# An S5, attention and convolution backbone step: S products in row halves with q slabs between, K and Y in column halves, the adaLN gate by DMA

## The reference, cut to what matters

```python
shift, scale, gate = split(silu(cond) @ w_ada + b_ada)
h = rmsnorm(x) * (1 + scale) + shift
z = h @ w_in                     # conv, ssm, q, k, v, gates, merge
br_a = (conv_module(z) * silu(conv_gate)) @ w_conv_out     # depthwise conv, width 31
# S5: 32 groups of 16 channels, 64 complex states, two directions
hs = scan(lam_bar, b_bar @ u);  y = d * u + real(c @ hs)
br_b = (glu(gelu(y)) * silu(ssm_gate)) @ w_ssm_out
br_c = (attention(qnorm(q), knorm(k), v) * silu(attn_gate)) @ w_attn_out
x = x + gate * ((g_a*br_a + g_b*br_b + g_c*br_c) @ w_out)
```

## Time and profile before

| what | value |
| --- | --- |
| median of 3 runs | 691.57 us (690.62 to 692.12) |
| profiled execution | 691.89 us, span 690.1 us |
| TensorE busy | 643.8 us, 93% |
| VectorE busy | 535.7 us, 78% |
| ScalarE busy | 309.6 us, 45% |
| GpSimd busy | 80.4 us, 12% |
| mean granted clock of TensorE | 0.989 |

### The profile page before, as it was taken

How to read it: one execution, slowest core, us unless ns; L and a number is a source line. 1 busy time by engine, 2 the same in 40 slices (tenths; PEclk the granted TensorE clock), 3 DMA queues, 4 the chain that set the end, 5 groups by cost and what they waited for, 6 DMA issues and landing times.

```text
span 690.1 us, 9683 instructions
## 1 busy us (share of the span) xinstructions
PE 643.8 (93%) x3573; PEld 460.7 (67%) x3573; DVE 535.7 (78%) x996; ACT 309.6 (45%) x534; POOL 80.4 (12%) x81
## 2 busy tenths in 40 slices
PE   3699799998999999999999899999999999989997
PEld 1377674554745688877887587465565578878885
DVE  2669889996676967789966837999767799987663
ACT  2665350540545354444546636044256544445441
POOL 2100220147000000010001710012700000010000
PEclk9999999999999999999999999999999999999999
DMA  7991817654583655655443337570443345655531
GB/s 263 373 315 58 264 60 230 238 186 119 174 284 120 180 160 173 183 162 153 162 149 113 116 137 267 179 258 29 151 151 106 106 127 184 199 163 181 184 102 61
DMA packets 67307, 117.66 MB, mean 171 GB/s; under 512 B 11052, under 2 KB 15484, under 8 KB 67260
## 3 DMA queue, kind: packets, MB, share of 16 engines
q1 hardware_dynamic: 66980, 116.94, 52.9%
q10 hardware_dynamic: 280, 0.11, 0.1%
HBM read 112.51 MB, written 1.38 MB: 165 GB/s over the span
## 4 chain that ended last, share of the span: by engine, by line
PE 72%; DVE 12%; SPq 6%; ACT 3%; issue 3%; DMA 2%; POOL 1%; ACTq 0%; POOLq 0%; DVEq 0%
PE proj L816 19%; PE proj L844 11%; PE proj L846 11%; PE proj L845 11%; PE side L831 4%; PE side L987 3%; PE side L974 2%; PE side L1068 2%; DVE raw_split L1506 2%; PE long L786 2%; PE side L1016 2%; SPq L629 1%; PE proj L786 1%; PE side L1066 1%; DMA raw<-in_w_in 1%
## 5 line engine op out<-in xcount | busy, mean ns | idle before, releaser
L816 PE MATMUL proj<-raw,hT 128*128 128x512 f32 (+1 forms) x320 | 132.0, 558 | 0.0
L1609 DVE SCALAR_TENSOR_TENSOR cvacc<-cvpad,taps,cvacc 128x256 f32<-128x256 f32 x240 | 99.0, 478 | 0.2
L816 PEld LDWEIGHTS proj<-raw,hT 128*128 128x128 f32 x320 | 58.2, 190 | 58.8 <-issue 57.0
L1212 ACT ACTIVATE wide_split<-raw 128x1024 fp32r<-128x1024 f32 x56 | 58.7, 1060 | 56.2 <-PE proj L846 56.2
L1506 DVE TENSOR_TENSOR raw_split<-raw,wide_split 128x1024 fp32r<-128x1024 f32 x56 | 67.8, 1221 | 17.2 <-ACT wide_split L1212 16.5
L845 PE MATMUL proj<-raw_split,H_split 128*128 128x512 f32 x192 | 75.5, 393 | 0.0
L844 PE MATMUL proj<-wide_split,H_split 128*128 128x512 f32 x144 | 57.9, 402 | 4.2 <-DVE raw_split L1506 4.2
L846 PE MATMUL proj<-wide_split,H_split 128*128 128x512 f32 x144 | 56.9, 395 | 0.0
L1212 ACT ACTIVATE utok_split<-raw 128x1024 fp32r<-128x1024 f32 x28 | 29.6, 1058 | 34.5 <-PE proj L846 34.5
L1506 DVE TENSOR_TENSOR raw_split<-raw,utok_split 128x1024 fp32r<-128x1024 f32 x28 | 34.2, 1221 | 12.3 <-ACT utok_split L1212 12.3
L2010 POOL TENSOR_SCALAR st<-st 128x1 f32<-128x1 f32 x8 | 4.6, 571 | 332.5 <-DVE st L1924 251.8
(11 more groups left out here) (255 smaller groups left out, 1377.6 us busy)
## 6 DMA issues: line engine op xcount, KB each, us to landing
raw<-in_w_in SPq DMA_DIRECT2D x104, 512.0 KB, 4.5
raw<-in_w_ada SPq DMA_DIRECT2D x48, 512.0 KB, 5.4
raw<-in_w_out SPq DMA_DIRECT2D x16, 512.0 KB, 3.8
raw<-in_w_ssm_glu SPq DMA_DIRECT2D x8, 512.0 KB, 7.1
raw<-in_w_ssm_out SPq DMA_DIRECT2D x8, 512.0 KB, 3.8
raw<-in_w_attn_out SPq DMA_DIRECT2D x8, 512.0 KB, 4.2
raw<-in_w_conv_out SPq DMA_DIRECT2D x8, 512.0 KB, 3.7
raw<-in_w_in SPq DMA_DIRECT2D x8, 256.0 KB, 3.6
```

The lines of the kernel that those rows point to most:

```text
L816: m = T.matmul(proj.bank((l, u, s))[:, 0:n], lhs[:, s, kt, :], w[:, i, :], start=(kt == 0), stop=last)
L1212: S.activation(piece_room[m], piece_raw(m), ACT.Copy).then_inc(piece_hi, 1)
L1609: m = V.scalar_tensor_tensor(acc, src, taps[:, t, j:j + 1], acc, ALU.mult, ALU.add)
```

## The change

S becomes one product per group: 64 rows of `E` against the 64 columns of its own group, the even group in the upper half of the rows and the odd one in the lower, into two banks at a time. Behind each of the first three pairs of banks TensorE works one slab of q and its ada slab; the q stage keeps the last. K and Y put groups in the two halves of the output partitions, K in four banks instead of eight. HY makes all four quarters before Y, the last two in `tA` and `tB`. The counts of taps per place change. The gate third of the adaLN output is no longer transposed: GpSimd adds the bias in row form (`gaterow`), and SP spreads the rows over 128 partitions by DMA into `th`; the bias comes by two DMAs into `taprow`, ahead of the q slabs in SP's queue. The waits that go with these places change too: b_loads wait for Y, `adaE` waits for `gaterow`, `bbar` for the last gate load, and GpSimd clears `taprow` at the start.

```diff
@@ -48,11 +48,11 @@
 EARLY = ("cg", "ssm", "ca")
 LATE_ROOMS = 3
 
-TAPS_IN_ZONE = (26, 14)
-TAPS_IN_Y = (8, 5, 6)
+TAPS_IN_ZONE = (22, 12)
+TAPS_IN_Y = 12
 TAPS_IN_ATT = (((8, 8, 4, 4, 2), (4, 4, 4, 4, 0)), ((6, 6, 3, 3, 2), (4, 4, 4, 4, 0)))
 
-CONV_B = (12, 18)
+CONV_B = (14, 20)
 
 LAST_COMB = ("comb", BRANCHES[-1], 1)
 
@@ -75,9 +75,9 @@
                  ("bbar", l), ("unit", "ca"), ("pack",)]
     return (begin
             + [("UT",), ("S",), ("cp",), ("bz", 0), ("convT", 0), ("convT", 1), ("unit", "q"), ("unit", "kv"), ("adaE", l, 2),
-               ("K", 0), ("sumsq", 0), ("sumsq", 1), ("unit", "sg"), ("bz", 1), ("K", 1), ("scan", 0, NCHUNK), ("HY",),
-               ("unit", "ag")] + nxt("adaE", n, 0)
-            + [("qkn",), ("conv", TAPS_IN_ZONE[l], None), ("Y",), ("adaT", l, 2)] + nxt("adaT", n, 0)
+               ("K", 0), ("sumsq", 0), ("sumsq", 1), ("bz", 1), ("unit", "sg"), ("K", 1), ("gaterow",), ("scan", 0, NCHUNK),
+               ("HY",), ("unit", "ag")] + nxt("adaE", n, 0)
+            + [("qkn",), ("conv", TAPS_IN_ZONE[l], None), ("Y",)] + nxt("adaT", n, 0)
             + [("qkT", 0), ("qkT", 1), ("att", 0)] + nxt("adaE", n, 1)
             + [("geT",), ("att", 1), ("unit", "glub"), ("unit", "glua"), ("split", 0), ("split", 1)]
...
@@ -319,12 +318,15 @@
         HY, HYs = shared("HY", [P, 2, 8, 2, NS, NCHUNK])
         HYf = HY[:, :, :, :, :, :].rearrange("p a g r s k -> p a (g r s k)")
         Ug = HY[0:NS * NCHUNK].rearrange("p a g r s k -> p (a g r s k)")
+        states = [HY[:, 0], HY[:, 1]] + [t[:, :].rearrange("p (g r s k) -> p g r s k", g=8, r=2, s=NS) for t in (tA, tB)]
         geT = HYf[:, 0, :].rearrange("p (s t q) -> p s t q", s=NS, t=WT)
         utok, utoks = shared("utok", [P, NS, W])
         cvpad = sb("cvpad", [P, WT, NS, P + 2 * PAD])
         cvacc, cvaccs = shared("cvacc", [P, WT, NS, P])
         taps = sb("taps", [P, WT, TAPS + 1])
         taprow = sb("taprow", [P, W])
+        biasrow = taprow[:, 0:ADA_W]
+        gaterow = bzf[:, 0:ADA_W]
         rows = sb("rows", [P, 3, W])
         modrow = rows[:, 0, 0:P]
...
@@ -647,9 +655,27 @@
 
             def tap_loads(l):
                 if l:
-                    side.filled(sp, ("taps", l - 1))
+                    sp.wait_ge(gaterow_done, l)
                 sp.dma_start(taprow[0:TAPS, :], A["conv_dw_w"][l]).then_inc(taps_in, 16)
                 sp.dma_start(taprow[TAPS:TAPS + 1, :], A["conv_dw_b"][l:l + 1, :]).then_inc(taps_in, 16)
+
+            def bias_loads(l):
+
+                side.filled(sp, ("taps", l))
+                for s in range(NS):
+                    sp.dma_start(biasrow[s::P // ADA_TILES, :],
+                                 A["b_ada"][l, 2 * D:3 * D].rearrange("(j x) -> j x", x=ADA_W)).then_inc(bias_in, 16)
+
+            def gate_rows(l, h):
+
+                sp.wait_ge(gaterow_done, l + 1)
+                for s in range(NS):
+                    key = (l, "gate" + str(h), s)
+                    th_claim(sp, key)
+                    for i in range(2):
+                        row = P // ADA_TILES * (2 * h + i) + s
+                        sp.dma_start(th_view(key)[:, ADA_W * i:ADA_W * i + ADA_W],
+                                     gaterow[row:row + 1, :].unsqueeze(1).to_broadcast([1, P, ADA_W])).then_inc(gate_in, 16)
 
             def c_loads(l):
...
@@ -745,6 +772,8 @@
                         b_loads(l + 1)
                         c_loads(l + 1)
                         tap_loads(l + 1)
+                    if stg[0] == "wout" and i == 3:
+                        gate_rows(l, stg[1])
                     if n >= first:
                         slab(n)
...
@@ -964,28 +993,34 @@
                     side.drained(pe, ("E", l, 5))
                     side.drained(pe, ("E", l, 6))
                     side.drained(pe, ("E", l, 7))
-                    for i in range(8):
-                        key = ("S", l, i)
-                        side.claim(pe, key)
-                        out = side.bank(key)[:, :].rearrange("p (g a r q) -> p g r a q", g=2, a=2, r=2)
-                        for gg in range(2):
-                            gp = 2 * i + gg
+                    for i in range(4):
+                        keys = [("S", l, 2 * i + a) for a in range(2)]
+                        for key in keys:
+                            side.claim(pe, key)
+                        for gp in range(4 * i, 4 * i + 4):
                             for r in range(2):
-                                m = T.matmul(out[:, gg, r, :, :], E[:, r, gp, :], Uz[:, 2 * gp:2 * gp + 2, :],
-                                             start=True, stop=True)
-                        m.then_inc(side.full, 1)
+                                for a in range(2):
+                                    at = 64 * (2 * (gp % 4) + r)
+                                    m = T.matmul(side.bank(keys[a])[:, at:at + 64], E[64 * a:64 * a + 64, r, gp, :],
+                                                 Uz[64 * a:64 * a + 64, 2 * gp + a, :], start=True, stop=True)
+                                    if gp == 4 * i + 3 and r == 1:
+                                        m.then_inc(side.full, 1)
+                        if i < 3:
+                            for key in [(l, "q", i)] + riders(l, "q", i):
+                                slab_work(key)
                 elif k == "K":
                     half = stg[1]
                     pe.wait_ge(cp_done, 2 * (l + 1))
                     pe.wait_ge(bz_done, 2 * l + half + 1)
-                    for i in range(4 * half, 4 * half + 4):
+                    for i in range(2 * half, 2 * half + 2):
                         key = ("K", l, i)
                         side.claim(pe, key)
                         for b in range(4):
-                            g = 4 * i + b
                             for r in range(2):
-                                m = T.matmul(side.bank(key)[0:48, 80 * b:80 * b + 80], bz[:, r, g % 16, :],
-                                             CP[:, r, :, g, :], start=(r == 0), stop=(r == 1))
+                                for a in range(2):
+                                    g = 8 * i + 4 * a + b
+                                    m = T.matmul(side.bank(key)[64 * a:64 * a + 48, 80 * b:80 * b + 80], bz[:, r, g % 16, :],
+                                                 CP[:, r, :, g, :], start=(r == 0), stop=(r == 1))
                         m.then_inc(side.full, 1)
                 elif k == "qkT":
                     s = stg[1]
@@ -1060,13 +1095,15 @@
                         side.claim(pe, key)
                         pe.wait_ge(hy_fwd, 4 * l + q + 1)
                         pe.wait_ge(hy_bwd, 4 * l + q + 1)
-                        for gi in range(8):
-                            g = 8 * q + gi
-                            o = side.bank(key)[0:64, 64 * gi:64 * gi + 64]
-                            T.matmul(o, Uz[:, g, :], M[:, :, g // 2, :], start=True, stop=False)
+                        for i in range(4):
+                            gs = [4 * q + i, G // 2 + 4 * q + i]
+                            out = [side.bank(key)[64 * a:64 * a + 64, 64 * i:64 * i + 64] for a in range(2)]
+                            for a in range(2):
+                                T.matmul(out[a], Uz[:, gs[a], :], M[:, :, gs[a] // 2, :], start=True, stop=False)
                             for r in range(2):
-                                m = T.matmul(o, HY[:, q % 2, gi, r, :, :].rearrange("p s k -> p (s k)"),
-                                             CP[:, r, 1:L + 1, g, :], start=False, stop=(r == 1))
+                                for a in range(2):
+                                    m = T.matmul(out[a], states[q][:, 4 * a + i, r, :, :].rearrange("p s k -> p (s k)"),
+                                                 CP[:, r, 1:L + 1, gs[a], :], start=False, stop=(r == 1))
                         m.then_inc(side.full, 1)
                     key = ("fin", l)
...
@@ -1092,17 +1129,6 @@
                     for t in range(WT):
                         m = transpose(side.bank(key)[:, P * t:P * t + P], src[:, P * t:P * t + P])
                     m.then_inc(side.full, 1)
-                if k == "wout":
-                    h = stg[1]
-                    side.drained(pe, ("adaT", l, 2))
-                    for s in range(NS):
-                        key = ("gate", l, h, s)
-                        side.claim(pe, key)
-                        for i in range(4):
-                            col = ada[:, l, 2 * DT + 4 * h + i, s:s + 1]
-                            m = T.matmul(side.bank(key)[:, P * i:P * i + P], col.to_broadcast([P, P]), ident[:, :],
-                                         start=True, stop=True)
-                        m.then_inc(side.full, 1)
                 if k == "pass":
                     u, s, h = stg[1:]
...
@@ -1187,8 +1213,8 @@
 
             def states_fwd(q):
 
```

(73 more changed lines are left out.)

51 lines of the change are left out of this document (27 added, 24 removed).

## The result

The changed kernel takes 739.05 us (737.15 to 739.5, 4 executions) against 691.85 for the kernel before in the same measurement: ratio 1.068, 95% interval [1.065, 1.070]. Forecast were 698.3 us and a range of 690.8 to 712.6. The sign was right; the size was off by 41 us, and nearly all of that is one term, the gates by DMA.

What follows compares the result with a forecast made beforehand. The prediction took TensorE (72% of the chain) as the bound, with VectorE taking over between S and attention. Terms 0.8 + 0.4 + 5.0 + 3.2 + 2.8 - 5.5 = +6.7 us gave a 698.3 us median, range 690.8 to 712.6.

Steps and rivals of the forecast that it cites:

- Gates by DMA: In both `wout` stages, TensorE's gate products and ScalarE's copies vanish: -5.5 us, bounds 2.9 to 7.2.
- S itself: S in row halves: 64 pairs at 112 ns, 7.2 us, unchanged, if row halves overlap as column tiles do.
- (a): Rival on S: half-row loads follow one another, S takes 14.3 us, +14.2, so 712.5 us; chance 0.16.
- (b): Rival on S: half-row products with their loads cost half, S 3.6 us, -7.2, so 691.1 us; chance 0.10.
- The 0.4 us for the bias loads: Layer 0: bias loads ahead in SP's queue make the first q slab late: +0.4 us, bounds 0 and 1.
- `cp` 13.5 us later behind S's start: Slabs inside S (12.6 us) and one more drain (0.9 us) delay VectorE's `cp` products in each layer.
- VectorE's taps set the first scores: Taps run unbroken to 182 and 510, TensorE idling 8 us or more; first scores +0.8 and +5.0 us.
- GpSimd caught by the taps: GpSimd's k norm product of stream 1 ends only with VectorE's taps; the norm's rest then takes 2.1 us.
- K and Y count nothing: Column halves of K and Y are covered by VectorE's chain: 0 us; without cover up to 10 a layer.
- The clock: TensorE's idle before stream 1's transposes brings one clock dip in each attention: +3.2 us, bounds 0 and 6.8.
- rival (c): The waits are there, but the clock holds and the rooms absorb the taps: 692.3 us; chance 0.14.
- Taps in the branches: Layer 1's branches take more taps, 3.6 us less VectorE's idle: +2.8 us, bounds 0 and 3.6.

Runs made afterwards that it cites:

- ky_halves_dram: The kernel before with K and Y in column halves and the gates by DMA from rows written to DRAM first: 674.53 us (0.976).
- ky_halves_only: The kernel before with K and Y in column halves, with the four state copies in a row this needs, and nothing else: 679.51 us (0.983).
- via_dram: The changed kernel with the gate rows first written to DRAM and spread over 128 partitions from there: 703.74 us (1.017).
- pe_gate: The changed kernel with the gates made by TensorE and copied by ScalarE as before, all other edits kept: 704.64 us (1.018).
- own_row: The changed kernel with each gate load reading source row p for target row p, not one row for all 128: 703.26 us (1.015).
- s_whole_between: The changed kernel with gates by TensorE and S at full height, q slabs still between its pairs of banks: 699.14 us (1.011).
- s_first: The changed kernel with gates by TensorE and the three q slabs behind S instead of between its pairs: 696.88 us (1.008).
- before_dma_gate: The kernel before with the gates by DMA alone, nothing else changed: 721.65 us (1.044).
- s_between_only: The kernel before with S in row halves, q slabs between its pairs and the changed tap numbers; K and Y full width, gates by TensorE: 709.94 us (1.025).
- s_halves_only: The kernel before with S in row halves alone, its pairs one behind the other: 714.2 us (1.033).
- taps_back: The changed kernel with gates by TensorE and the kernel before's numbers of taps, q slabs still inside S: 713.81 us (1.032).
- s_first_taps: The changed kernel with gates by TensorE, q slabs behind S and the kernel before's numbers of taps: 698.41 us (1.009).

## Why the prediction was wrong

**The step that failed** is in "Gates by DMA": SyncE "issues four loads, some 0.6 us each, ahead of one w_out slab, which still lands before ScalarE asks for it". The median issue was 0.60 us, but landing took 7.2 to 21.4 us, and the slab came 11.4 us after ScalarE asked. The term was -5.5; in the changed kernel it is +34.4 (739.05 - 704.64). I had priced the loads by their issue and never asked how long they hold the DMA engines. The trace of before had no load with a single source partition in SBUF; that made it a cost to bound from both sides, and I bounded only the gain, 2.9 to 7.2. Its own `rows<-in_ssm_d` spreads a DRAM row over 128 partitions, 256 KB landing in 3.2 us, and was no row for this one.

**The gain of 5.5 itself** was too large by a little, as far as the runs tell. Where the source is not the fault, ky_halves_dram against ky_halves_only has 5.0 us, with intervals that overlap; via_dram against pe_gate has 0.9, own_row 1.4, though in both S of layer 1 ran under a dip of 6.8 us that pe_gate's did not. The two stretches that hold a `wout` are, added up, 4.6 us shorter in via_dram's profile than in pe_gate's, and 4.5 shorter in ky_halves_dram's than in ky_halves_only's.

**S itself: right.** 16 pairs take 2.00 us at full clock, 125 ns a pair against 112 (before, 115 an instruction):

```profile
97.84 2.00 PE L1004 MATMUL side<-Uz,EC 64*128 64x64 f32 x32
99.78 3.70 PE L845 MATMUL proj<-raw,hT 128*128 128x512 f32 x8
103.41 0.64 PE L815 MATMUL long<-raw,cond 128*32 128x256 f32 x8
```

So rivals (a), 220, and (b), 60, both fall. At full height the same products take 2.05 us in s_whole_between: the halves save nothing. That holds between slabs; with nothing between, the same instructions took 3.68 us (s_first). The 0.4 us for the bias loads did not show: TensorE had no wait for a slab of q in layer 0.

**`cp` 13.5 us later behind S's start: right in layer 1, short in layer 0.** It starts 22.40 us behind S's start against 8.52 before, +13.9, and 26.80 against 10.14 in layer 0, +16.7. There the clock was low for 10.2 us from 86.2, and the first pair and slab took 3.68 and 6.42 us.

```profile
463.76 1.23 DVE L1530 TENSOR_TENSOR tA<-cT,lamr 128x1024 f32<-128x1024 f32 x1
```

**VectorE's taps set the first scores: right.** They ended at 187.36 and 533.17. TensorE waited 9.17 us for it in layer 0 ("idle 8 us or more") and in layer 1 1.13 us for the k norm and then 5.35:

```profile
187.77 1.30 PE L860 MATMUL side<-ident,qk 128*128 128x128 f32 x5 [9.17 <-DVE ada L1530]
...
533.64 1.19 PE L1051 MATMUL side<-kz,qM 128*128 128x256 f32 x2 [5.35 <-DVE kz L1892]
```

The stretches to the first scores grew by 4.7 and 5.0 us; the terms for them were 0.8 + 0.4 and 5.0 (the 1.6 for a dip lies behind the first scores). So layer 0 was 3.5 us short, and the hit in layer 1 was luck: behind S's start the taps ended 2.5 us later than the sum had them (5.0 in layer 0), and the 2.4 us of k norm behind the taps, next paragraph, did not come.

**GpSimd caught by the taps: wrong.** In both layers of the changed kernel it got through; its 128x128 product, begun among the taps, took 0.52 us, against 11.36 and 6.60:

```profile
174.34 0.52 POOL L2026 TENSOR_TENSOR qk<-qk,qst 128x128 f32<-128x128 f32 x1
```

In pe_gate, layer 0, the same product took 11.35 us and ended 0.3 us behind the last tap, just as forecast:

```profile
171.69 11.35 POOL L2042 TENSOR_TENSOR qk<-qk,qst 128x128 f32<-128x128 f32 x1
```

It cost 1.70 us there. Over all the runs the pattern is plain: where HY has two copies before the taps (before, before_dma_gate, s_between_only, s_halves_only) it was caught in 8 of 8 layers; where it has four, in 1 of 24. I had reasoned that two more copies bring the taps late enough to catch it; they let it go. What goes with it in all 32 layers is the offset: the 23 products that got through began 1.25 to 1.26 us behind the first tap, the 9 that were caught 2.31 to 5.34. In pe_gate's layer 0 the offset was 2.31; an earlier instruction of GpSimd (`qst<-qst,st`) had taken 5.41 us there and 3.60 in the changed kernel. The rule of the Trainium skill that the prediction leaned on (SBUF — State Buffer, Who interferes with whom) makes the port that the two share an exclusive lock; that doesn't forbid GpSimd to get a turn between two taps. By that rule, the trace agrees: while GpSimd's instructions run, the taps of the changed kernel start 0.46 to 0.60 us apart, else 0.40. Why an early start lets it through stays open.

**K and Y count nothing: wrong in the step, harmless in the sum.** I said that at full width Y would end near 182 and 506.5. In s_between_only it ended at 186.0 and 520.2, with TensorE last: 5.3 us over pe_gate. (Its HY has two copies before Y and two within, so this is K, Y and that order together.) Since the change halves them, they are covered and add nothing to its sum. The prediction gave them up to 10 us a layer without that cover. With S left alone the cover is gone: first scores come 10.2 and 4.7 us sooner behind S's start, and the time falls by 11.5 us, the largest gain in the change. In K 64 instructions take 2.42 us where they took 4.63, in Y each takes 29 ns where they took 57:

```profile
122.76 2.42 PE L1017 MATMUL side<-EC,bz 128*48 128x80 f32 x64
```

**The clock: right in kind.** The cover gone, dips stood around both first scores: 181.8 to 192.0 in layer 0. In 184 to 188 TensorE has one instruction and the lower clock:

```profile
184.00:188.00 4.00, 0.23 (x1) 0.26 (x2) 3.90 (x13) 0.00 (x0) 0.00 (x0) 0.50 0.04 11
```

Before, the gaps were shorter, and a dip stood behind Y's. Each of the two dips at the first scores costs about half of what lies behind the first scores, 1.5 us; 1.6 was the term. So rival (c) falls too: the clock did not hold. It was low for 84 us of the span in all (15 before), 34 of them in four dips in the two layers' `wout`, where TensorE starved for weights.

**Taps in the branches: too large.** pe_gate's last stretch is 185.72 us against 182.13. Of the 3.6 us, half of two clock dips (the last 1.8 us of one and 3.4 us) is 2.6; about 1.0 is left for the taps, within the bounds of 0 and 3.6, and taps_back, which takes them out again, gave back 1.5. The term was 2.8.

So the direction came from the right chain. That pe_gate's 704.6 meets the 704.1 of the sum without its gate term is in part luck: the stretches to the first scores grew by 2.9 and 5.7 us where the sum had 0.8 and 5.0, and what lies behind them (dips, taps in the branches) by 4.0 where it had 6.0. The rivals were all about S; none was about the edit that had no row.

## What to carry to other kernels

Price a transfer by how long it holds the DMA engines, not by its issue: a row in SBUF spread over 128 partitions runs at 27 GB/s and stops every weight behind it. Write such a row to DRAM and spread it from there, or keep copies in partitions far apart (here 0, 8, 68 and 84). And test the edits of a package one by one: here the halving of K and Y, with the copies that go with it, gives -11.5 us, hidden under an S in row halves that saved nothing and a reordering that made VectorE late. An operation between two steps may be what keeps banks drained and the clock up.

## What the runs showed of the hardware

- From one SBUF partition, or four neighbours, all 16 DMA engines together read 26 to 35 GB/s, at 80 to 87% busy; from DRAM the same 128 KB landed in 3.8 us beside weight loads instead of 14.7.
- A run of 128 S instructions of 64 rows and 64 columns, with waits of 1.17 us between groups of 32, ran at the lower clock for 17 to 24 us in six of six layers (s_first, s_first_taps, s_halves_only). At full height, without such waits, 64 instructions had 7.38 us in ky_halves_only's layer 0. Whether it was the halves or the waits is not told apart.
- GpSimd's 128x128 product beside VectorE's taps takes either 0.52 us or until the run of taps ends (4.6 to 11.4 us); both occur in one program (pe_gate, 11.35 us in layer 0 and 0.52 in layer 1). It took 0.52 in the 23 layers where it began 1.25 to 1.26 us behind the first tap, and the long time in the 9 where it began 2.31 us behind it or later.
